# A new order inside the sample-attention loop of a hybrid decoder step: scores and weights ahead of the next key transposes

## What is computed

```python
def mla_sample(q_nope, q_rope, ckv_new, kr_new, cache_lat, cache_kr, page_table, w_uk, w_uv):
    lat_past = cache_lat[page_table].reshape(Bd, -1, MLA_KV_RANK)      # 8 x 4096 x 128
    kr_past = cache_kr[page_table].reshape(Bd, -1, MLA_ROPE)           # 8 x 4096 x 32
    q_lat = jnp.einsum('bshn,rhn->bshr', q_nope, w_uk)
    s_past = jnp.einsum('bshr,btr->bhst', q_lat, lat_past) + jnp.einsum('bshp,btp->bhst', q_rope, kr_past)
    ...
    p = jax.nn.softmax(s, axis=-1).astype(lat_all.dtype)
    o_lat = jnp.einsum('bhst,btr->bshr', p, lat_all)
    return jnp.einsum('bshr,rhv->bshv', o_lat, w_uv)
```

## Time and profile before

| what | value |
|---|---|
| median of 3 runs | 799.71 us (796.49 to 801.13) |
| the profiled execution | 799.71 us |
| its span in the profile | 797.9 us |
| outside the span | 1.8 us |
| sample loop, from the start of T(2) to the end of `values_out(15)` | 598.6 to 671.9 us |
| PE busy over the whole span | 92% |

### The profile page before, as it was taken

One profiled execution on the slowest core, in us unless ns is written; L12 is line 12 of the kernel. 1 busy time (PEld: TensorE's weight loads), 2 busy tenths in 40 slices (PEclk: granted clock), 3 DMA queues, 4 the chain that ended last, 5 costly groups with the idle time before them and its releaser, 6 DMA issues.

```text
span 797.9 us, 16962 instructions
## 1 busy us (share of the span) xinstructions
PE 731.0 (92%) x7069; PEld 558.1 (70%) x7069; DVE 359.2 (45%) x750; ACT 331.9 (42%) x785; POOL 91.9 (12%) x112
## 2 busy tenths in 40 slices
PE   1699999999999989999989999999979898899994
PEld 1296777878789966777755677766669886377883
DVE  0371260020101035877667567666721112398886
ACT  2070561024112145776545456556746563611010
POOL 0000000000000020110121202101023330202220
PEclk9799999999999979999999999999999998699997
DMA  9992110203001010000000200201128990112222
GB/s 318 414 320 104 64 42 1 104 1 87 1 10 44 27 45 15 9 15 14 6 8 0 54 1 1 53 3 67 68 92 297 363 379 20 55 39 101 99 105 79
DMA packets 31508, 70.29 MB, mean 88 GB/s; under 512 B 6418, under 2 KB 20843, under 8 KB 28364
## 3 DMA queue, kind: packets, MB, share of 16 engines
q1 hardware_dynamic: 27242, 47.73, 17.8%
q0 software_dynamic: 3584, 20.97, 6.9%
q10 hardware_dynamic: 610, 0.55, 0.3%
HBM read 62.26 MB, written 6.07 MB: 86 GB/s over the span
## 4 chain that ended last, share of the span: by engine, by line
PE 78%; DVE 8%; DMA 6%; ACT 3%; issue 2%; SPq 2%; POOL 1%; DVEq 0%; ACTq 0%; POOLq 0%
PE banks L1800 27%; PE banks L2332 8%; PE banks L1997 8%; PE banks L2055 4%; PE banks L2136 3%; DMA s_z<-in_cache_k_rope,s_idx 3%; DMA s_x<-in_x_prompt 3%; PE banks L2158 3%; PE banks L1966 2%; PE banks L1903 2%; DVE s_w_out_lo L1679 1%; PE banks L2227 1%; PE banks L2247 1%; PE banks L1879 1%; PE banks L1841 1%
## 5 line engine op out<-in xcount | busy, mean ns | idle before, releaser
L941 ACT ACTIVATE s_z<-banks 128x506 f32<-128x506 f32 (+3 forms) x48 | 24.4, 513 | 160.4 <-PE banks L1800 160.4
L2332 PE MATMUL banks<-s_out_parts 128*128 128x512 f32 x256 | 81.0, 395 | 3.8 <-DVE s_w_out_lo L1679 2.8
L1800 PE MATMUL banks<-s_w_parts,s_h_a 128*128 128x256 f32 (+3 forms) x352 | 79.8, 327 | 0.3 <-DVE s_h_a L1289 0.3
L1800 PE MATMUL banks<-s_w_parts,s_h_b 128*128 128x256 f32 (+3 forms) x352 | 79.6, 327 | 0.0
L1800 PE MATMUL banks<-s_z_r,s_h_a 128*128 128x506 f32 (+2 forms) x224 | 72.9, 391 | 0.0
L1800 PE MATMUL banks<-s_z_r,s_h_b 128*128 128x506 f32 (+2 forms) x224 | 72.8, 390 | 0.0
L1317 DVE COPY s_front<-banks 128x506 f32<-128x506 f32 (+3 forms) x6 | 3.5, 588 | 136.9 <-PE banks L1766 136.9
L1141 ACT ACTIVATE s_z<-banks 128x512 f32<-128x512 f32 (+1 forms) x88 | 41.3, 517 | 52.4 <-PE banks L2136 52.3
L2332 PEld LDWEIGHTS banks<-s_out_parts 128*128 128x128 f32 x256 | 48.6, 190 | 16.7 <-issue 4.0
L1800 PEld LDWEIGHTS banks<-s_w_parts,s_h_b 128*128 128x128 f32 x352 | 52.7, 189 | 7.5 <-issue 1.5
L1800 PEld LDWEIGHTS banks<-s_w_parts,s_h_a 128*128 128x128 f32 x352 | 52.8, 189 | 7.1 <-issue 1.9
(11 more groups left out here) (339 smaller groups left out, 1318.2 us busy)
## 6 DMA issues: line engine op xcount, KB each, us to landing
s_z<-in_w_ada SPq DMA_DIRECT2D x8, 1024.0 KB, 19.5
s_x<-in_x_prompt SPq DMA_DIRECT2D x8, 512.0 KB, 21.5
s_z<-in_w_ada SPq DMA_DIRECT2D x1, 4096.0 KB, 15.9
s_kt<-in_w_out SPq DMA_DIRECT2D x8, 512.0 KB
s_temps<-in_x_prompt SPq DMA_DIRECT2D x8, 512.0 KB
out_y_prompt<-s_temps SPq DMA_DIRECT2D x8, 512.0 KB
s_temps<-in_w_in SPq DMA_DIRECT2D x2, 2024.0 KB, 7.8
s_temps<-in_w_in SPq DMA_DIRECT2D x2, 1024.0 KB, 5.4
```

What stands on the lines that cost most here:

```text
L941: nc.scalar.activation(z[:, t, EDGES[c]:EDGES[c + 1]], banks[:, t % 6, 0:n], func).then_inc(proj_copied, 1)
L1800: last = nc.tensor.matmul(banks[:, t % 6, 0:EDGES[c + 1] - EDGES[c]], h_[half][:, k, n0:n0 + P], w_[c][:, k, :], start=(k == 0 and n == 0) ...
L2332: last = nc.tensor.matmul(banks[:, 2 * u + q, :], m_[u][:, k, :], w_[:, k, 512 * q:512 * q + 512], start=(k == 0 and n == 0), stop=(k == K ...
```

## The change

Three places change. On **PE** T(n+2) moves, inside iteration n, from the front to behind `scores(n+1)`, so that only `weighted(n)` comes after it. On **ACT** `weights(n+1)` moves from behind the five copies of step n+2 to behind the first two. On **POOL** the second wait of a gather asks for one more maximum: `f_mx` at n-2, so `largest(n-3)` and no longer `largest(n-4)`. No instruction is added or removed, and no shape or buffer changes.

```diff
@@ block.gpsimd
             for n in range(UNITS, NSTEPS):
                 pool.wait_ge(f_o, n - UNITS + 1)
-                pool.wait_ge(f_mx, n - 3)
+                pool.wait_ge(f_mx, n - 2)
                 gather(n)
@@ block.scalar
             weights(0)
             for n in range(NSTEPS):
                 if n + 2 < NSTEPS:
-                    for j in range(5):
+                    for j in (0, 1):
                         keys_out(n + 2, j)
                 if n + 1 < NSTEPS:
                     weights(n + 1)
+                if n + 2 < NSTEPS:
+                    for j in (2, 3, 4):
+                        keys_out(n + 2, j)
@@ block.tensor
             for n in range(NSTEPS):
-                if n + 2 < NSTEPS:
-                    all_transposed(n + 2)
                 weights_transposed(n)
                 if n + 1 < NSTEPS:
                     scores(n + 1)
+                if n + 2 < NSTEPS:
+                    all_transposed(n + 2)
                 weighted(n)
```

## The result

The changed kernel takes **810.45 us** (median of 20 runs, 803.87 to 815.49), the kernel before 799.82 us beside it (20 runs). The ratio is **1.0127, with a 95% interval of 1.0103 to 1.0150**: slower by about 10.2 us, where 798.2 us and no measurable difference had been forecast. The time lies outside the range of 795.5 to 803.5.

What follows compares the result with a forecast made beforehand. PE was taken to bound the sample loop's steady state. Entry order -1.3, clock -1.5, steady state +2.9 and gather waits -1.6 sum to -1.5 us, so 799.7 becomes 798.2 us, range 795.5 to 803.5.

Steps and rivals of the forecast that it cites:

- The entry: Start of the sample loop: small transpose and scores of step 1 fit ahead of T(2), -1.3 us; clock stays full, -1.5 us.
- They are hidden: At the entry, `weights_transposed(0)` and `scores(1)` are done at 597.7, before T(2) starts at 598.6; gain -1.3 us.
- The rival of the late semaphore: At the entry, `largest(0)` starts late at 600.60 again and PE waits for it; 803.0 us, chance 0.26.
- The steady state: Each loop iteration: PE waits 0.21 us for ACT's last copy before the scores, period 4.76 us; 14 x 0.21 = +2.9 us.
- a mere change of order inside the iteration can't shorten it: Sample loop: PE has no idle row in its 4.55 us period, so reordering inside an iteration gains nothing there.
- The waits for gathers: T's waits for gathers in the loop: 1.6 us instead of 3.2, so -1.6 us, bounds 0 and -3.2.
- the earlier weight pieces: SP's output weight pieces start 2.4 us earlier, where DMA engines weren't full, so gather 8 lands between 627.2 and 630.0.
- the loop runs later than the gathers' pace: Later in the loop, T(7) and T(13) start late enough to need no wait for their gathers.
- The end: From T(15) to the loop's end: 8.0 us instead of 9.26, the entry's 1.3 seen again and not counted twice.
- period above 4.9: Sign of failure: the prediction fails if the loop's period is above 4.9 us, against 4.76 forecast.
- to 14 x 0.3: Upper bound of the steady-state term, if PE's restart behind a semaphore costs another 0.1 us.

Runs made afterwards that it cites:

- entry_old: Changed kernel with T(2) first again at the entry, the new order from iteration 1 on; 803.65 us, ratio 1.0067 to the kernel before.
- no_gathers_new: Changed kernel without the gathers of steps 5 to 15, which work on rows of an earlier step; period 4.87 us.
- rot_on_dve: Changed kernel with the rotary copy, ACT's fifth of each step, moved to DVE; 808.06 us, ratio 1.0103 to the kernel before.
- switches: Kernel before without gathers of steps 5 to 15, the four rotary transposes put between scores and `weighted`; period 4.83 us.
- gather_on_sc: Changed kernel with POOL's second wait on the scores (`f_sc`) instead of the maximum; 806.07 us, ratio 1.0057 to the kernel before.
- w_out_early: Kernel before with each piece of the output weights started two steps earlier; 799.71 us, ratio 0.9970 to the kernel before.
- f_mx_old: Changed kernel with POOL's old second wait, `f_mx` at n-3; 810.32 us, ratio 1.0149 to the kernel before.
- burst_split: Changed kernel with gathers 3 and 4 held back until `largest(0)` is done; 807.98 us, ratio 1.0132 to the kernel before.
- issue2: Two kernels: kernel before without gathers of steps 5 to 15, one small indirect DMA a step instead, issued on `f_o` or `f_pT`; period 4.54 us in both.
- issue3: Both issue2 kernels run again unchanged on another chip; every period 4.54 us.

## Why the prediction was wrong

**The entry, forecast -1.3 (order) and -1.5 (clock): wrong, and the step that failed was the choice between two cases that were both seen.** "They are hidden" rested on `largest(0)` starting on time. The forecast set the late start in the earlier trace rows aside with two arguments: that the other 15 maxima are prompt, and that PE's next instruction no longer waits for a DMA. The first says nothing here, since no other maximum has six issues in a row beside it. The second is refuted: the maximum is as late in the changed kernel, where PE's next instruction waits for no DMA (5.4 us), as in entry_old, where it does (5.3 us). The rival of the late semaphore, with a chance of 0.26, describes what happened: T(2) behind the scores, a half-clock stretch, its T done at about 606.6 by the old clock. Measured, that T (from 608.48 to 612.20, with `scores(0)` 4.3 us later in this run) ends at 607.9 on that scale. The entry is +5.7 and the end -1.3, so the net is +4.4 where the rival had +2.9. entry_old shows it: with T(2) first again, 4.3 us come back. Most of what the rival lacked is the clock: three items and not one ran at half (1.94 instead of 1.08 for 32 products, 0.66 instead of 0.40, 3.35 instead of 1.97), 2.5 us and not 1.5.

**The steady state, forecast +2.9: the direction was right, largely by luck, and the term mis-sized by a factor of 2.4 (6.0 against 2.5 over the 12 periods).** The forecast's whole reason was a wait for ACT, and of the growth ACT's part is the smallest. The wait for ACT was worked out correctly: the scores start 3.64 us behind T. What was wrong is the other side of that difference, PE's own arrival, which I put at 3.43 by adding up durations of the old order. It is 3.60 (no_gathers_new and rot_on_dve). The sentence that a mere change of order inside the iteration can't shorten it took for granted that it can't lengthen PE's own work either. It does, by 0.29 us: the earlier trace rows holds two changes between wide transposes and narrow products, and the new order has four. switches shows it with ACT out of the way. ACT's part is 0.04 us, not 0.21.

**What no term held: the gathers' issue beside `weighted`, +0.19 us a period.** I worked out when POOL would issue (0.85 us behind T; measured 1.19) in order to know when the gather lands, and never asked what PE does while POOL issues. The issue moved from beside the transposes to beside the products. gather_on_sc gets most of it back. The three parts, 0.29 + 0.04 + 0.19 = 0.52, are the whole growth of the period shown above (5.06 against 4.54; in the other runs with an issue beside `weighted` it is 4.96 to 5.16). Twelve of them are 6.2 us, and the table has 6.0, since a step whose T waited for a gather has POOL done before `weighted` (641.19 to 646.07, 4.88 us).

**The waits for gathers, forecast -1.6: right in kind, -1.0 measured**, inside its bounds. Their places were not: 1.11 at T(8), 0.28 at T(13) and 0.96 at T(14), where T(8) alone had been forecast. Of the two reasons given, w_out_early does not bear out the earlier weight pieces, which alone gain nothing. The other, that the loop runs later than the gathers' pace, fits f_mx_old, which has no such wait at all and a slower loop, but no run tests it by itself.

**The end, 8.00 us: right** (forecast 8.0).

Summed up, the forecast of the loop was -1.5 and it is +9.4: of the 10.9 us between, 6.8 lie at the entry and the end together (+4.4 against -2.8 and two periods' 0.4), 3.5 in the 12 periods (6.0 against 2.5) and 0.6 in the waits. The chances were wrong as well as the value: the larger part of the miss lay in a rival that I had priced, and the "period above 4.9" that would make the prediction fail was named but given no weight. Nor was there a term for a cost that the trace of before could not show, which is what the bounds "to 14 x 0.3" should have covered; 14 x 0.52 is 7.3.

## What to carry over

When an order is changed, the durations from the old timeline hold only between the same neighbours: count the changes between kinds of work on the engine that bounds (here 0.14 us for each change between 128-column and 32-column work on PE), and price each new seam. A late start with an unexplained releaser in the trace of before is a fact about the kernel; if a change puts something behind that start, take it as late until a run shows otherwise. And where a DMA is issued by POOL, look at what PE does in that moment, and not only at when the data land.

No version tried that still gathers the rows of every step beats the kernel before. With the gathers of steps 5 to 15 left out, the loop of the old order takes 74.4 us in its one run instead of 77.9; so all its waits for gathers behind the entry together are worth no more than about 4 us.

## What the runs showed of the hardware

- PE's semaphore for finished work came 4.9 to 5.4 us late where POOL issued six indirect DMAs in a row, and 0.7 to 0.8 us behind the end of a pair of issues that had run beside 32-column products; where ACT waits for PE too, it is late until the same moment as DVE (burst_split, f_mx_old). The products themselves can be slowed (2.64 us for 0.99). In four runs of two kernels (issue2, issue3) the same burst at the same place held nothing. The Trainium skill ("SBUF — State Buffer", Who interferes with whom) states that PE and ACT never wait on anyone; that is said of SBUF ports, and no run here tests the ports. Whatever path it takes, PE did not get through undisturbed here.
- A change between 128-column transposes and 32-column products cost about 0.14 us (4.83 us with four changes a period, 4.54 with two), seen as 0.17 to 0.20 us of idle time ahead of PE's weight loads.
- In the changed kernel the clock was at half (1.2 GHz) from 604.5 to 611.4, 6.8 us; it fell while PE stood, late in the stand of 6.19 us. In the kernel before it was at half for 3.4 us, from 598.4, late in the stand of 3.35. In burst_split T(2) still ran at full clock behind two stands of 0.90 and 0.94 us, as the forecast had assumed for such stands; behind two more, of 0.67 and 1.13 us, the clock did fall, for 3.4 us from 603.8.
